# Two banks for scores and three for maxima, a later row item, and the first output-projection splits inside the attention

## The reference

```python
proj = jnp.einsum('bsd,dc->bsc', x, w_in)
...
o_a = _gated_deltanet(...)            # 4 heads of 128, chunks of 64
y_a = rmsnorm(o_a) * silu(z_a)
o_b = _forgetting_attention(...)      # 8 heads of 64, causal softmax with a forget bias
y_b = o_b * silu(z_b)
mix = jnp.concatenate([y_a, y_b], axis=-1)
sub = jnp.einsum('bsc,cd->bsd', mix, w_out)
hres = DEEP_ALPHA * x + sub
out = LayerNorm(hres) * ln_g + ln_b
```

## Time and profile before

| | us |
|---|---|
| median of 3 runs | 1612.64 (1612.24 to 1614.11) |
| profiled execution, whole | 1609.38 |
| its span in the trace | 1607.6 |
| TensorE busy in the span | 1547.3 (96%) |
| VectorE busy | 923.3 (57%) |
| ScalarE busy | 691.5 (43%) |
| GpSimd busy | 622.6 (39%) |

### The profile page before, as it was taken

The page is one execution under the profiler, slowest core; times in us unless marked ns, Lnnn a source line. Parts: engine busy times, 40 slices in busy tenths (PEclk is TensorE's granted clock), DMA queues, the critical chain, the costliest instruction groups (busy, mean ns, idle before and its releaser), DMA issues. The chain is left out here.

```text
span 1607.6 us, 22182 instructions
## 1 busy us (share of the span) xinstructions
PE 1547.3 (96%) x7890; PEld 1224.3 (76%) x7890; DVE 923.3 (57%) x1436; ACT 691.5 (43%) x1307; POOL 622.6 (39%) x540
## 2 busy tenths in 40 slices
PE   7999999999999999999979999998999999979998
PEld 6888888888888888888856676666766677667886
DVE  7464555555317766901256776666667676545755
ACT  0436363645411111131125776765676777830100
POOL 1212021211311111111036787877786887911111
PEclk9999999999999999999979999999999999989999
DMA  6134344252573334226544645453546455324642
GB/s 254 49 118 144 96 119 128 88 156 72 157 117 125 131 118 131 72 70 140 158 136 130 186 118 148 141 145 93 145 125 180 119 149 169 88 76 115 200 138 92
DMA packets 190657, 206.49 MB, mean 128 GB/s; under 512 B 50940, under 2 KB 134140, under 8 KB 187516
## 3 DMA queue, kind: packets, MB, share of 16 engines
q1 hardware_dynamic: 189972, 203.24, 44.2%
q10 hardware_dynamic: 576, 1.84, 0.4%
HBM read 129.79 MB, written 75.17 MB: 127 GB/s over the span
## 5 line engine op out<-in xcount | busy, mean ns | idle before, releaser
L1487 POOL TENSOR_TENSOR m_p_lo<-m_p,m_p_hi 128x512 fp32r<-128x512 f32 (+1 forms) x320 | 373.9, 1190 | 61.1 <-ACT m_p_hi L1451 59.7
L545 PE MATMUL bank<-x_hi,w_hi 128*128 128x512 f32 x992 | 394.3, 397 | 0.0
L545 PE MATMUL bank<-x_hi,w_lo 128*128 128x512 f32 x992 | 387.1, 390 | 0.0
L545 PE MATMUL bank<-x_lo,w_hi 128*128 128x512 f32 x992 | 386.2, 389 | 0.0
L570 POOL TENSOR_TENSOR w_lo<-w_raw,w_hi 128x512 fp32r<-128x512 f32 x64 | 92.9, 1473 | 481.0 <-ACT w_hi L628 481.0
L1449 ACT ACTIVATE m_p<-m_st,fcol 128x512 f32<-128x512 f32 (+1 forms) x320 | 204.2, 638 | 153.9 <-PE m_st L1336 77.3
L1539 DVE TENSOR_REDUCE m_maxima<-m_aux 128x1 f32<-128x512 f32 (+2 forms) x320 | 195.3, 619 | 122.1 <-PE m_aux L1311 73.6
L545 PEld LDWEIGHTS bank<-x_hi,w_lo 128*128 128x128 f32 x992 | 186.2, 188 | 40.1
L545 PEld LDWEIGHTS bank<-x_lo,w_hi 128*128 128x128 f32 x992 | 186.6, 188 | 36.4
L545 PEld LDWEIGHTS bank<-x_hi,w_hi 128*128 128x128 f32 x992 | 186.4, 188 | 36.2
L1451 ACT ACTIVATE m_p_hi<-m_st,fcol 128x512 fp32r<-128x512 f32 (+1 forms) x320 | 202.5, 633 | 0.0
(11 more groups left out here) (204 smaller groups left out, 2522.3 us busy)
## 6 DMA issues: line engine op xcount, KB each, us to landing
w_raw<-in_w SPq DMA_DIRECT2D x31, 512.0 KB, 3.9
dram_feat<-ring SPq DMA_DIRECT2D x48, 256.0 KB, 4.2
arena<-dram_gates SPq DMA_DIRECT2D x32, 256.0 KB, 4.9
o_y<-dram_mixT SPq DMA_DIRECT2D x16, 512.0 KB, 6.1
o_x<-in_x SPq DMA_DIRECT2D x16, 512.0 KB, 4.1
out<-o_res SPq DMA_DIRECT2D x15, 512.0 KB, 5.0
arena<-in_xT SPq DMA_DIRECT2D x7, 1024.0 KB, 8.7
K<-dram_k_hi SPq DMA_DIRECT2D x12, 512.0 KB, 7.2
```

What stands on the lines that cost most here:

```text
L545: mm = pe.matmul(banks[bank_of(s)][:], w[:, i % 2, k * P:(k + 1) * P], x[:, k, b * BLOCK:(b + 1) * BLOCK], start=(k == 0 and n == 0), stop ...
L1487: pool.tensor_tensor(p_lo[(s - 1) % PL][:, off:], p[(s - 1) % PL][:, off:], p_hi[(s - 1) % PH][:, off:].bitcast(F32), ALU.subtract).then_i ...
```

## The change

It has five parts.

1. PSUM in mix: ST goes from 3 to 2, the aux banks from 2 to 3. scores(s) now needs p_hi of unit s - 2, and aux item m needs VectorE to be done with item m - 3.
2. The row item of a group stands three slots behind its last max item instead of two, on TensorE, and so does VectorE's copy of the row.
3. RESCALE goes from 16 to 15: VectorE's yb and the store of yb are a slot earlier in both queues.
4. The splits of w_out's first tile and of y's first tile move from the start of project_out into the last seven slots of mix: w_hi0 at slot 313 and y_hi0 at slot 316 on ScalarE, w_lo0 at slot 315 and y_lo0 at slot 318 on VectorE. SP's end of mix waits for both low parts. w_hi and w_lo become a tile for each k, and tiles of the output stage are laid at other places.
5. At the kernel's start, ScalarE waits for the first half of the first weight tile before it issues its DMA of the second weight tile.

```diff
-            for n in ("x", "h"):
-                scr["o_" + n] = [ahead.enter_context(nc.sbuf_tensor(f"o_{n}{i}", [P, D_MODEL], F32)) for i in range(2)]
+            scr["o_x"] = [ahead.enter_context(nc.sbuf_tensor("o_x0", [P, D_MODEL], F32))]
+            for n, shape in (("w_hi", [P, D_MODEL]), ("w_lo", [P, D_MODEL]), ("y_hi", [P, KT, P])):
+                scr["o_" + n] = [ahead.enter_context(nc.sbuf_tensor(f"o_{n}0", shape, F32R))]
...
+                act.wait_ge(w0_landed[0], 16)
                 act.dma_start(raw_of(1), io["w"][W_OF[ORDER[1][0]](ORDER[1][1])]).then_inc(w_landed, 16)
...
-ST, PH, PL = 3, 4, 3
+ST, PH, PL = 2, 4, 3
+AUX_BANKS = 3
 LEAD = 20
-SPREAD, INVERT, GATHER, SPREAD_BACK, RESCALE = 1, 6, 7, 11, 16
+SPREAD, INVERT, GATHER, SPREAD_BACK, RESCALE = 1, 6, 7, 11, 15
...
+FIRST_SPLIT = N_UNITS - 7
...
-            put(min(slot_of(n - 1) + 2, first_unit(G) - 1) if G else -1, ("row", G))
+            put(min(slot_of(n - 1) + 3, first_unit(G) - 1) if G else -1, ("row", G))
...
-        aux = [bank(f"aux{i}") for i in range(2)]
+        aux = [bank(f"aux{i}") for i in range(AUX_BANKS)]
         st = [bank(f"st{i}") for i in range(ST)]
...
-                            sp.dma_start(scr["o_w_raw"][k][:], io["w_out"][k]).then_inc(out_landed, 16)
+                            sp.dma_start(scr["o_w_raw"][k][:], io["w_out"][k]).then_inc(out_landed if k else w0_raw_landed, 16)
...
-                              .then_inc(out_landed, 16)
+                              .then_inc(out_landed if t else y0_landed, 16)
...
-                sp.wait_ge(out_landed, 12 * 16)
+                sp.wait_ge(out_landed, 10 * 16)
+                sp.wait_ge(first_lo, 2)
...
-                    b = aux[m % 2]
-                    done(pe, aux_used, m - 2)
+                    b = aux[m % AUX_BANKS]
+                    done(pe, aux_used, m - AUX_BANKS)
...
+                    if s == FIRST_SPLIT:
+                        act.wait_ge(w0_raw_landed, 16)
+                        done(act, aux_used, AUX_INDEX["max", N_GROUPS - 1, 3, NB - 1])
+                        act.activation(w_hi0[:], scr["o_w_raw"][0][:], ACT.Copy).then_inc(first_hi, 1)
+                    if s == FIRST_SPLIT + 3:
+                        act.wait_ge(y0_landed, 16)
+                        act.activation(y_hi0[:], scr["o_y"][0][:], ACT.Copy).then_inc(first_hi, 1)
...
+                    if s == FIRST_SPLIT + 2:
+                        dve.wait_ge(first_hi, 1)
+                        dve.wait_ge(scores_ready, last_unit(N_GROUPS - 3) + 1)
+                        dve.tensor_tensor(w_lo0[:], scr["o_w_raw"][0][:], w_hi0[:].bitcast(F32), ALU.subtract).then_inc(first_lo, 1)
+                    if s == FIRST_SPLIT + 5:
+                        dve.wait_ge(first_hi, 2)
+                        dve.tensor_tensor(y_lo0[:], scr["o_y"][0][:], y_hi0[:].bitcast(F32), ALU.subtract).then_inc(first_lo, 1)
...
-        w_hi = sb("w_hi", [P, KT, D_MODEL], F32R)
-        w_lo = sb("w_lo", [P, KT, D_MODEL], F32R)
+        w_hi, w_lo = (scr["o_" + n] + [sb(f"{n}{k}", [P, D_MODEL], F32R) for k in range(1, KT)] for n in ("w_hi", "w_lo"))
...
                 for k, t in FIRST_STEPS:
-                    pe.wait_ge(w_split, k + 1)
-                    pe.wait_ge(y_lo_ready, t + 1)
+                    if k > 0:
+                        pe.wait_ge(w_split, k)
+                    if t > 0:
+                        pe.wait_ge(y_lo_ready, t)
                     step(t, k)
...
-                high_w(0)
-                high_y(0)
                 high_w(1)
...
-                low_w(0)
-                low_y(0)
                 low_w(1)
```

More of the change, by code:

```diff
@@ L1075, in mix @@
                       for n, w in (("v_lo", FD), ("v_hi", FD + 1)))
+        scr["o_y_lo"] = [scr["shared"].enter_context(nc.sbuf_tensor("o_y_lo0", [P, KT, P], F32R))]
         for name, shape in (("den", [1, 512]), ("dens", [FD, 512 // FD]), ("recs", [FD, 512 // FD]), ("rec_b", [FD, 512]),
@@ L1079, in mix @@
             scr[name] = scr["shared"].enter_context(nc.sbuf_tensor(name, shape, F32))
-        out_landed = sem("out_landed")
+        out_landed, w0_raw_landed, y0_landed, first_hi, first_lo = (sem(n) for n in (
+            "out_landed", "w0_raw_landed", "y0_landed", "first_hi", "first_lo"))
+        w_hi0, w_lo0, y_hi0, y_lo0 = (scr["o_" + n][0] for n in ("w_hi", "w_lo", "y_hi", "y_lo"))
         ones = sb("ones", [P, FD])
@@ L1658, in project_out @@
         w_raw = scr["o_w_raw"]
-        w_hi = sb("w_hi", [P, KT, D_MODEL], F32R)
-        w_lo = sb("w_lo", [P, KT, D_MODEL], F32R)
+        w_hi, w_lo = (scr["o_" + n] + [sb(f"{n}{k}", [P, D_MODEL], F32R) for k in range(1, KT)] for n in ("w_hi", "w_lo"))
         ln_g, ln_b = sb("ln_g", [P, D_MODEL]), sb("ln_b", [P, D_MODEL])
         y = scr["o_y"]
-        y_hi = [sb(f"y_hi{i}", [P, KT, P], F32R) for i in range(WIDE)]
-        y_lo = [sb(f"y_lo{i}", [P, KT, P], F32R) for i in range(WIDE)]
-        x, h = scr["o_x"], scr["o_h"]
+        y_hi, y_lo = (scr["o_" + n] + [sb(f"{n}{i}", [P, KT, P], F32R) for i in range(1, WIDE)] for n in ("y_hi", "y_lo"))
+        x = scr["o_x"] + [sb("x1", [P, D_MODEL])]
+        h = [sb(f"h{i}", [P, D_MODEL]) for i in range(2)]
         scaled = scr["o_scaled"] + [sb("scaled1", [P, D_MODEL])]
@@ L1690, in load_y @@
                 def load_y(t):
-                    sp.wait_ge(y_lo_ready, t - WIDE + 1)
+                    if t > WIDE:
+                        sp.wait_ge(y_lo_ready, t - WIDE)
                     if t == 8:
@@ L1746, in step @@
                             cut = slice(c * 512, (c + 1) * 512)
-                            mm = pe.matmul(banks[t % WIDE][:, cut], a[t % WIDE][:, k, :], b[:, k, cut],
+                            mm = pe.matmul(banks[t % WIDE][:, cut], a[t % WIDE][:, k, :], b[k][:, cut],
                                            start=(k == 0 and n == 0), stop=(k == KT - 1 and n == 2))
@@ L1771, in high_y @@
                         act.wait_ge(summed, t - WIDE + 1)
-                        act.wait_ge(y_lo_ready, t - WIDE + 1)
+                        if t > WIDE:
+                            act.wait_ge(y_lo_ready, t - WIDE)
                     act.activation(y_hi[t % WIDE][:], y[t % WIDE][:], ACT.Copy).then_inc(y_hi_ready, 1)
                 def high_w(k):
-                    act.activation(w_hi[:, k, :], w_raw[k][:], ACT.Copy).then_inc(w_hi_ready, 1)
-                high_w(0)
-                high_y(0)
+                    act.activation(w_hi[k][:], w_raw[k][:], ACT.Copy).then_inc(w_hi_ready, 1)
                 high_w(1)
@@ L1796, in low_y @@
                 def low_y(t):
-                    dve.wait_ge(y_hi_ready, t + 1)
+                    dve.wait_ge(y_hi_ready, t)
                     if t >= WIDE:
@@ L1803, in low_w @@
                 def low_w(k):
-                    dve.wait_ge(w_hi_ready, k + 1)
-                    dve.tensor_tensor(w_lo[:, k, :], w_raw[k][:], w_hi[:, k, :].bitcast(F32), ALU.subtract)\
+                    dve.wait_ge(w_hi_ready, k)
+                    dve.tensor_tensor(w_lo[k][:], w_raw[k][:], w_hi[k][:].bitcast(F32), ALU.subtract)\
                        .then_inc(w_split, 1)
-                low_w(0)
-                low_y(0)
                 low_w(1)
```

## The result

The changed kernel takes 1603.28 us in the median (1602.21 to 1605.36, 4 runs) against 1612.72 (1612.24 to 1614.11, 4 runs) before: a ratio of 0.9942, 95% interval 0.9924 to 0.9959, or 9.4 us less (6.6 to 12.3). Forecast were 1588.8, 24 us less, with a range up to 1604. The direction held, the size did not, and the time lies just inside the range's far end. Its profiled execution took 1603.56 us (span 1601.7), so the two traces stand 5.8 us apart where the medians stand 9.4 apart: the trace of before is of an execution 3.3 us under its median.

A forecast was written before the change was run, and what follows sets the result against it. TensorE was taken as the bound, with only waits and clock to win. Terms -16.5 - 3 + 0.5 - 2 + 0.5 - 0.1 - 3.2 = -23.8 us gave 1588.8 us from 1612.6, range 1578 to 1604.

The forecast's parts named there:

- The bound, the view, the sign: TensorE sets the end with its work unchanged; waits and clock can be won, 23.8 us less in all.
- Third aux bank and score banks: In mix, aux matmuls' 4.5 + 3.0 us of waits for VectorE nearly all go; two score banks cost +0.5 us.
- The score banks: Scores in mix need p_hi of unit s - 2; waits only here and there, +0.5 us, between 0 and +5.
- Rival (c): Two score banks tie TensorE to ScalarE, losing 0.1 us a unit over 320 units: 1620 us, slower; chance 0.11.
- The row item: In mix, its 5.6 + 1.0 us of waits for GpSimd's diagonal nearly all fit in one slot more.
- The clock: Dips at 990 and 1145 us may go with the small waits ahead of them: -2 us, between -5 and +5.
- Rescale a slot earlier: VectorE in mix waits longer for rec_b, the third bank takes one item of it: +0.5 us, between 0 and +4.
- QM's loads: The 5.02 us query-tile load wait at 1105.11 stays; at 1173.82 TensorE waits for such a load instead, 1.1 us.
- Splits and boundary: Last slots of mix: stage end -0.1 us; first steps of project_out after the barrier: -3.2 us.
- The start: ScalarE's wait before its first DMA at kernel start changes nothing: 0 us, between -1.1 and +1.5.
- (a): Freed TensorE meets p_lo or QM load waits instead: -9 to -12 us, some 1602 us; chance 0.18.
- parts 1 and 2: Aux banks and row item in mix: -16.5 us from 843 to 1400 us, -3 in the first units.

The follow-up runs named there:

- banks alone: Two score banks and three aux banks put into the kernel before, nothing else: ratio 0.9922, 12.6 us less.
- two score banks alone: The kernel before with two score banks and two aux banks, one PSUM bank unused: ratio 0.9988.
- keys later: The changed kernel with the loads of the next head's keys six slots later in SP's queue: ratio 0.9895 of the kernel before.
- splits alone: The kernel before with part 4's first splits in the attention's last slots and its tiles laid anew, nothing else: ratio 0.9997, 0.5 us less.
- banks and row: The kernel before with two score banks, three aux banks and the row item a slot later, nothing else: ratio 0.9938.

## Why the prediction was wrong

**The bound, the view, the sign:** right. TensorE's work stayed the same and the gain is in waits.

**Third aux bank and score banks:** right and undersized. 7.5 us of named waits, 11 with all that I added, measured 12.6 (9.4 to 15.6) by banks alone. The score banks, +0.5, cost nothing (two score banks alone, -1.9, interval -3.9 to +0.2). Rival (c), the slower one, is refuted.

**The row item:** wrong, and this is the step that failed: "So nearly each of these waits fits in what it is given", with the 1.2 us taken off for p_lo. The sum had some -8 us for this item. Measured, it gives about +2.5 beside the banks (intervals that overlap, so no gain can be shown) and +7 (4.7 to 9.2) without them. The row item itself no longer waits. But it waited for GpSimd, and GpSimd's p_lo of the next unit stands behind the same m_max_diag: at seven places 6.2 us of the row item's wait became 5.1 us of waits for p_lo, which went from 5.3 us in banks alone to 10.9. I had followed TensorE past the moved step and not asked what else GpSimd gives out behind the instruction that was waited for. Smaller in sum, but with the clock behind it, is the second half of the row item, VectorE's copy, which moved too: up against m_so, for which GpSimd stands in order with p_lo behind it (0.7 us more at 886 us, then 6.8 us at 1.2 GHz). The views to read would have been GpSimd's own waits: in the trace of before, 36.4 us in 24 places for m_mcol and 25.1 in 13 for m_so stand ahead of p_lo in its queue. I had read that GpSimd was busy 76.84 of 100 us and asked whether it had work enough to be late, not what it waits for.

**The clock:** -2 forecast, +3.5 in the pair of traces. The dip at 990 went as hoped; waits of 1.4 to 2.4 us brought two new ones and made the one at 1145 longer. The range had it (up to +5), the centre did not: I had let the waits that come back be short ones, with no fall of the clock behind them.

**Rescale a slot earlier:** sign right, size wrong. +0.5 forecast; +4.5 (1.3 to 7.6) alone. In the changed kernel VectorE waits 13.7 us for the reciprocals instead of 3.7; I named the wait, and let the third bank hide it.

**QM's loads:** right for the 5 us that stay. The 1.1 us wait expected in the place of 1173.82 did not come.

**Denominators behind the keys:** not in my sum. A 2 KB transfer of 9.2 us was in the trace of before; with TensorE 8 us earlier VectorE's wait for it grew from 3.4 to 6.1 us and reached TensorE. That is 5.9 us of the missing 14, a good part of it in the clock's term too. A transfer that is issued by slots comes sooner by what TensorE gained ahead of the issue, and lands after the same time; what is gained between issue and use shortens its cover.

**Splits and boundary:** the steps behind the barrier right to 0.1 us (0.04 and 3.24). The tail was sized by the wrong row: 0.44 us for each operation of VectorE, taken beside one that is half as long, measured some 1.0. Here the Trainium skill, page "SBUF — State Buffer", section "SBUF: two separate sides", was the better guide: whichever of the two comes second waits until the first is done. w_lo0, issued beside a p_lo that ended at 1402.51, took 2.30 us, and the p_lo behind it 2.2. The 2.4 us that I had worked out by that page for the two low parts stand against some 1.9 measured, and 0.9 by my row. The whole term, -3.3, counted in all traces from unit 316 to the end, is -3.2 in the changed kernel (-2.8 with the keys later) and -1.9 both in splits alone and in the changed kernel with RESCALE 16. So the traces bear the size out, about 1 us of it by the earlier rescale; the timing can't tell it from nothing.

**The start:** 0 forecast, 1.3 (-1.1 to +3.5) measured.

**The rivals:** what happened is (a), "The waits change their name", with 1602 for its time and 0.18 for its chance; the measurement is 1603.3. Its mechanism is the one measured for the row item. That its time came out so near is in part luck: it had 7 us for parts 1 and 2 and 2 for the boundary, where banks and row gave 10 (7.1 to 12.9), splits alone 0.5, and the earlier rescale took some back; and of its two reasons (p_lo, the QM load) only p_lo came, the load that came up was another. It ought to have had a larger chance: by the trace of before m_max_diag, which the row item waited for, stood in the same queue as p_lo.
